# Twenty conditioning products: GpSimd scales and adds the row slices of the weights, TensorE only sums over partitions

## The reference

```python
for i in range(DEPTH):                     # DEPTH = 2
    mod_l = silu(c) @ ada_w[i] + ada_b[i]      # c: 1 x 1024, ada_w[i]: 1024 x 6144
    mod_c = silu(c_ctx) @ ada_w[i] + ada_b[i]
    sh1_l, sc1_l, gt1_l, sh2_l, sc2_l, gt2_l = split(mod_l, 6)   # and so for mod_c
    ...
```

## Time and profile before

| | us |
|---|---|
| median of 3 runs | 3075.93 |
| lowest, highest | 3074.19, 3077.70 |
| profiled execution, its span | 3075.3 |
| PE busy in it | 2984.1 |
| DVE busy | 1734.7 |
| ACT busy | 715.3 |
| GpSimd (POOL) busy | 77.7 |

### The profile page before, as it was taken

One profiled execution on the slowest core, in us unless ns is written; L12 is line 12 of the kernel. 1 busy time (PEld: TensorE's weight loads), 2 busy tenths in 40 slices (PEclk: granted clock), 3 DMA queues, 4 the chain that ended last, 5 costly groups with the idle time before them and its releaser, 6 DMA issues. The chain is left out here.

```text
span 3075.3 us, 53460 instructions
## 1 busy us (share of the span) xinstructions
PE 2984.1 (97%) x23086; PEld 2376.8 (77%) x23086; DVE 1734.7 (56%) x2567; ACT 715.3 (23%) x1371; POOL 77.7 (3%) x105
## 2 busy tenths in 40 slices
PE   8999999999999999999999999989999999999998
PEld 8988775559987998685558985655888887766897
DVE  5554456446556564464546556584333664486666
ACT  2102114222112101223322104282111012254210
POOL 1000000000001000000000000000000000001000
PEclk9999999999999999999999999999999999999999
DMA  8645403237656746313227744102222443231553
GB/s 288 223 175 184 142 30 110 97 110 234 206 183 196 260 164 216 134 60 108 99 83 234 237 141 151 55 1 83 82 82 83 150 154 113 98 122 63 165 165 110
DMA packets 279818, 429.94 MB, mean 140 GB/s; under 512 B 10072, under 2 KB 147776, under 8 KB 279584
## 3 DMA queue, kind: packets, MB, share of 16 engines
q1 hardware_dynamic: 273936, 411.52, 39.5%
q0 software_dynamic: 5024, 13.82, 1.4%
q10 hardware_dynamic: 624, 1.19, 0.1%
HBM read 425.45 MB, written 1.05 MB: 139 GB/s over the span
## 5 line engine op out<-in xcount | busy, mean ns | idle before, releaser
L460 PE MATMUL bank<-arena 64*64 64x64 f32 (+8 forms) x7292 | 740.9, 281 | 23.3 <-DVE arena L2069 4.6
L460 PE MATMUL bank<-xT,ring 128*128 128x128 f32 (+2 forms) x4512 | 725.1, 320 | 10.3 <-DVE arena L852 5.7
L460 PEld LDWEIGHTS bank<-arena 128*128 128x128 f32 (+3 forms) x7292 | 640.6, 161 | 120.1 <-issue 36.6
L460 PEld LDWEIGHTS bank<-xT,ring 128*128 128x128 f32 (+1 forms) x4512 | 657.7, 191 | 71.2 <-issue 10.5
L460 PE MATMUL bank<-ring,xT 128*128 128x512 f32 (+3 forms) x1648 | 577.2, 519 | 2.2 <-DVEq L2086 1.2
L460 PEld LDWEIGHTS bank<-ring,xT 128*128 128x128 f32 (+1 forms) x1648 | 264.0, 182 | 253.5 <-issue 237.0
L460 PE MATMUL bank<-ring,arena 128*128 128x256 f32 (+1 forms) x1584 | 436.9, 427 | 12.4 <-issue 5.3
L460 PEld LDWEIGHTS bank<-ring,arena 128*128 128x128 f32 x1584 | 298.2, 190 | 123.9 <-issue 82.0
L852 DVE TENSOR_TENSOR arena<-arena,bank 128x256 f32<-128x256 f32 (+1 forms) x198 | 92.2, 466 | 395.7 <-PE bank L460 254.7
L763 ACT COPY arena<-bank 128x256 f32<-128x256 f32 (+1 forms) x264 | 107.7, 408 | 747.2 <-PE bank L460 745.9
L812 DVE TENSOR_TENSOR arena<-ring,arena 128x1024 f32<-128x1024 f32 (+1 forms) x216 | 257.1, 1190 | 7.4
(11 more groups left out here) (421 smaller groups left out, 2186.8 us busy)
## 6 DMA issues: line engine op xcount, KB each, us to landing
ring<-in_ffn_w SPq DMA_DIRECT2D x88, 1024.0 KB, 8.0
ring<-in_w_in SPq DMA_DIRECT2D x32, 2048.0 KB, 7.7
ring<-in_ffn_w_in SPq DMA_DIRECT2D x44, 1024.0 KB, 6.5
arena<-in_ada_w SPq DMA_DIRECT2D x20, 2048.0 KB, 13.2
ring<-in_ffn_w SPq DMA_DIRECT2D x16, 2048.0 KB, 7.9
ring<-in_ffn_w_out SPq DMA_DIRECT2D x12, 2048.0 KB, 7.8
ring<-in_hgrn_w_in SPq DMA_DIRECT2D x12, 2048.0 KB, 7.9
ring<-in_ffn_w SPq DMA_DIRECT2D x8, 1536.0 KB, 6.6
```

The costliest lines, as they stand in the source:

```text
L460: return self.e.matmul(o, lhsT, rhs, start=start, stop=stop, skip_group_check=True)
```

## The change

Twenty products (still "home") get another form. For each half of the weights (four k) GpSimd multiplies the row slice k by silu(c)[k], a per-partition scalar out of `c_wide`, and adds it to a sum; the same for silu(c_ctx), if that row is needed (`ada_streams`: 14 of the 20 products need both, 6 one). PE then only sums over the partitions: 4 matmuls per row, with `pick` as weights (a column of ones among zeros, 32 columns wide). The sums lie alternately in the arena and in `xT`. The weights come in two halves, each reloaded when GpSimd has used it (`ada_half_used`); GpSimd raises `ada_summed` when a sum is complete, and waits for `ada_used` of the product two before. Marks and loads are redistributed: 3, 4, 4 and 5 products in the passes, 1, 2 and 1 in transitions; the four ring products stay in the transitions. The loads of halves follow `HOME_LOADS`: half h of a product is issued by SP h blocks after its number. GpSimd's program gets `pool_ada` in the passes; inputs of the mixer's second layer and of the embedding are issued behind the first sum of their pass. `ada_rows` has three buffers, and several semaphores are merged (`late_norms_landed`, `rows_landed`, `dve_step`).

```diff
-             "pick": (np.arange(15)[None, :] == 7) & (p >= 0),
+             "pick": (np.arange(63)[None, :] == 31) & (p >= 0),
...
-        ada_landed = sem("ada_landed")
+        ada_landed = [sem(f"ada_landed{h}") for h in range(2)]
+        ada_half_used = [sem(f"ada_half_used{h}") for h in range(2)]
+        ada_summed = sem("ada_summed")
...
+                def loaded():
+                    for h in range(2):
+                        if len(mine) - 1 - h in marks:
+                            modulation(h)
...
-                    if b in marks:
-                        modulation()
+                    loaded()
                 for half in range(2 * streams):
                     for k0 in range(0, FT, 8):
                         mine.append(blocks[0])
                         load((0, 0, k_rows(w_down, 512 * (half % 2), 512)[:, k0:min(k0 + 8, FT)]))
...
+                        loaded()
...
-            def modulation_at_home():
-                l2, c0 = next(ada)
-                if homes[0]:
-                    eng.wait_ge(ada_used, homes[0])
-                homes[0] += 1
-                eng.dma_start(f_ada[:], k_rows(a["ada_w_2"][l2], c0, 512)).then_inc(ada_landed, 16)
+                    m = next(ring_blocks)
+                    wide(a["ada_w_2"][m // 12], m % 12 * 512, 512)
+
+            def modulation_half(h):
+                m = ADA_HOME[homes[h]]
+                if homes[h]:
+                    eng.wait_ge(ada_half_used[h], homes[h])
+                homes[h] += 1
+                eng.dma_start(f_ada[:, 4 * h:4 * h + 4], k_rows(a["ada_w_2"][m // 12], m % 12 * 512, 512)[:, 4 * h:4 * h + 4]
+                              ).then_inc(ada_landed[h], 16)
...
-        ada_rows = at(arena_cols - 2 * P, 2, P)
-        ln_rows = at(arena_cols - 3 * P, P)
-        lb_rows = at(arena_cols - 3 * P, P)
-
-        IN_TRANSITION = ((2, 0, 1, 0), (2, 0, 0, 0))
-        IN_FFN = (((3, 5, 7, 8, 9), (3, 5, 7, 9)), ((3, 5, 7, 8, 9), (3, 5, 7, 8, 9)))
-        assert all(n % 2 == 0 or not m for t in IN_TRANSITION for n, m in enumerate(t))
-        assert sum(sum(n) for n in IN_TRANSITION) + sum(len(m) for n in IN_FFN for m in n) == ADA_BLOCKS
+        ada_rows = at(arena_cols - 3 * P, 3, P)
+        ln_rows = at(arena_cols - 4 * P, P)
+        lb_rows = at(arena_cols - 4 * P, P)
+
+        IN_FFN = (((5, 7, 9), (3, 5, 7, 9)), ((3, 5, 7, 9), (3, 5, 7, 9, 10)))
+        TRANSITION = ((("home", "ring", "ring"), (), ("home", "home"), ()), (("home", "ring", "ring"), (), (), ()))
+        HOME_LOADS = ((2, 4, 6, 8), (0, 2, 4, 6, 8, 10), (0, 2, 4, 6, 8), (0, 2, 4, 6, 8))
+        ADA_KINDS = [kind for l in range(DEPTH) for n in range(2)
+                     for kind in ("home",) * len(IN_FFN[l][n]) + TRANSITION[l][2 * n]]
+        ADA_HOME = [n for n, kind in enumerate(ADA_KINDS) if kind == "home"]
+        ADA_RING = [n for n, kind in enumerate(ADA_KINDS) if kind == "ring"]
+        assert len(ADA_KINDS) == ADA_BLOCKS and len(ADA_HOME) == sum(len(x) for x in HOME_LOADS)
+
+        def ada_streams(i):
+
+            n = ADA_HOME[i]
+            return (0, 1) if n // 12 == 0 or n % 12 < 4 else (0,)
+
+        def ada_sum(i, s):
+
+            if i % 2:
+                return xT[:, 4 + 2 * s:6 + 2 * s, SEQ:512]
+            return f_ada_sum[:, s].rearrange("p (a b) -> p a b", a=2)
+
+        ada_scaled = xT[:, 2:4, SEQ:512]
+
+        def pool_ada(pool, f, after_first=None):
+
+            e = pool.e
+            pool.wait_ge(x_sums, x_sums_before(f) + 1)
+            first = sum(len(x) for x in HOME_LOADS[:f])
+            for i in range(first, first + len(HOME_LOADS[f])):
+                if i >= 2:
+                    pool.wait_ge(ada_used, i - 1)
+                streams = ada_streams(i)
+                for h in range(2):
+                    pool.wait_ge(ada_landed[h], pool.due(ada_landed[h], 16))
+                    for k in range(4 * h, 4 * h + 4):
+                        w_ = f_ada[:, k].rearrange("p (a b) -> p a b", a=2)
+                        scaled = []
+                        for s in streams:
+                            last = s == streams[-1]
+                            out_ = ada_sum(i, s) if k == 0 else w_ if last else ada_scaled
+                            if last and len(streams) == 2:
+                                pool.wait_ge(pool_step, scaled[0])
+                            e.tensor_scalar(out_, w_, c_wide[:, k, s:s + 1], None, ALU.mult).then_inc(pool_step, pool.up(pool_step))
+                            scaled.append(pool.sent(pool_step))
+                        for s in streams:
+                            if k:
+                                pool.wait_ge(pool_step, scaled[s])
+                                acc = ada_sum(i, s)
+                                e.tensor_tensor(acc, acc, w_ if s == streams[-1] else ada_scaled, ALU.add
+                                                ).then_inc(pool_step, pool.up(pool_step))
+                        if k:
+                            pool.wait_ge(pool_step, pool.sent(pool_step) - len(streams) + 1)
+                    pool.wait_ge(pool_step, pool.sent(pool_step))
+                    pool.sem_inc(ada_half_used[h], pool.up(ada_half_used[h]))
+                pool.sem_inc(ada_summed, pool.up(ada_summed))
+                if i == first and after_first:
+                    after_first()
 
         def pe_ada_product(pe, home=False):
 
             if home:
-                pe.wait_ge(ada_landed, pe.due(ada_landed, 16))
-                blk = f_ada
-            else:
-                blk = pe.block()
+                pe.wait_ge(ada_summed, pe.due(ada_summed))
+                pe.wait_ge(to_act.freed, to_act.next_free())
+                bank = to_act.free_bank()
+                streams = ada_streams(pe.homes)
+                for s in streams:
+                    for j in range(4):
+                        mm = pe.mm(bank[32 * j:32 * j + 32, 0:P], pick[:, 31 - s:63 - s],
+                                   ada_sum(pe.homes, s)[:, j // 2, j % 2 * P:j % 2 * P + P], s == 0, s == streams[-1])
+                mm.then_inc(to_act.filled, 1)
...
+                pe.homes += 1
+                return
...
         def act_parameters(act):
+            act_ada_turn(act)
             act.sem_inc(ada_ready, act.up(ada_ready))
...
+            pool.wait_ge(late_norms_landed, pool.due(late_norms_landed, 48))
...
+            def mix_inputs(l):
                 if l:
                     pool.wait_ge(ln_used, pool.due(ln_used))
                 ln(l, 0)
-                pool_mix(pool, l)
+                pool_mix_rows(pool, l)
+
+            def embedding_inputs(l):
+                pool.wait_ge(ln_used, pool.due(ln_used))
+                ln(l, 2)
+                if l == DEPTH - 1:
+                    pool_second_inputs(pool)
+                pool_ple(pool, l)
+
+            for l in range(DEPTH):
+                if l == 0:
+                    mix_inputs(0)
+                pool_ada(pool, 2 * l, (lambda: mix_inputs(l)) if l else None)
+                pool_mix_lora(pool, l)
                 pool_gla(pool)
                 pool_gdn(pool)
-                for n in range(1, 4):
-                    if n > 1:
-                        pool.wait_ge(ln_used, pool.due(ln_used))
-                    ln(l, n)
-                    if n == 2:
-                        if l == DEPTH - 1:
-                            pool_second_inputs(pool)
-                        pool_ple(pool, l)
+                ln(l, 1)
+                pool_ada(pool, 2 * l + 1, lambda: embedding_inputs(l))
+                pool.wait_ge(ln_used, pool.due(ln_used))
+                ln(l, 3)
```

101 lines of the change are left out of this document (46 added, 55 removed).

## The result

The changed kernel takes 3365.9 us (median of 4 runs, 3361.4 to 3371.0) against 3075.2: a ratio of 1.094, 95% interval 1.093 to 1.096. It is slower by 291 us, and above the upper end of the predicted range (3260).

A forecast was written before the change was run, and what follows sets the result against it. PE's instruction stream, busy 97%, was taken as the bound, with PE then waiting at marks for GpSimd's sums: 3075.3 - 26.3 + 139.3 = 3188.3 us profiled, 3189 as the median of runs; range 3060 to 3260.

The forecast's parts named there:

- The scaling's price: GpSimd's scaling of 128x512 was taken at 0.65 us, so a two-row product alone at 28.8 us.
- (a): Rival: GpSimd keeps ahead, a two-row product under 26 us and not held by DVE; 3050 to 3065 us, chance 0.17.
- The port: GpSimd and DVE exclude each other at SBUF, making a two-row product 36.5 us against marks 25.9 us apart.
- the mixer's inputs: In the third pass their DMA issues and a memset behind GpSimd's first sum take 10.7 us.
- PE's gain: Shorter home products on PE save 39.5 us at marks, less 11.9 and 1.3: 26.3 us.
- the same work where PE and DVE don't wait: 0, up to 1 us: Other edits, such as late norms, wider pick, row buffers and the moved last turn, cost 0, up to 1 us.
- SP's order: Ring blocks wait in SP's queue behind unused halves; hidden in the 36.5 us while GpSimd is the bound.
- no charge: The two products in the transition after the second pass have some 93 us, need about 89, and cost nothing.
- Pass by pass: New waits of PE in the four feed-forward passes: 23.6, 44.4, 53.3 and 18 us, sum 139.3 us.
- The restart: PE may restart slowly after a long wait, but inside intervals that GpSimd sets.
- (b): Rival: GpSimd is not held by DVE but needs 28.8 us per two-row product; 3094 us, chance 0.12.
- if scalings measure 0.9 us or more, the top of the range: Sign for GpSimd's scalings: at 0.9 us or more the time would be at the range's top, 3260 us.

The follow-up runs named there:

- x5: The changed kernel with GpSimd's scalings multiplying by the constant 0.5 instead of a per-partition scalar read from SBUF: 3341.9 us, ratio 1.086.
- x13: The changed kernel with most scalings cut to 192 of their 512 columns, number and order of operations kept: 3245.4 us, ratio 1.055.
- y1: The kernel before, with four of the five products of the fourth pass summed by DVE with fused multiply-adds: 3074.75 us, ratio 0.9998.
- x1: The changed kernel with GpSimd's scalings after the first slice and all additions replaced by memsets of about equal length: 3274.6 us, ratio 1.064.
- x2: The changed kernel with GpSimd handling only the first of the eight row slices of each product: 3056.5 us, ratio 0.993.
- x4: The changed kernel with the halves of the conditioning weights loaded by GpSimd's own queue instead of SP's: 3390.4 us, ratio 1.102.
- x14: The changed kernel with the load of the second pass's last product two blocks later in SP's order: 3353.9 us, ratio 1.091.
- x8: The changed kernel with 56 idle matmuls on PE ahead of its wait for each home sum: 3452.6 us, ratio 1.123.

## Why the prediction was wrong

**The scaling's price: the step that failed.** "I take 0.65", between a memset (0.54) and the addition (1.10), as an operation that reads one tensor should lie between one that reads none and one that reads two. It takes 1.56 us alone, above the bound that the sum called its upper one, and the x5 run puts nearly all of it down to the operation itself. The addition, 1.10 in the earlier trace rows, takes 1.27 here, as the two in the earlier trace rows did (1.26, 1.27), which the sum had in hand and didn't use. One slice then takes 5.65 us (65.80 to 71.45 in the timeline) and a two-row product alone 8 x 5.65 - 2.5 (the first slice has no additions) + 0.6 (gaps) = 43.3 us for 28.8: 14.5 us more, eleven times, 160 us. All of it is the scaling's, 16 x 0.91 = 14.6: the additions are 2.4 us dearer than in the sum, and the waits of GpSimd for its own last instruction, 3.0 in the sum, are 0.6. Of the 177 us between the forecast and the result (3365.9 - 3188.9) that leaves 17. x13 shows the same from the other side: with the scaling at 0.76 us the kernel is 120 us faster. The bounds were drawn from the count of tensors read; neither row was of that operation, and the upper end should have gone beyond the nearest of them.

The Trainium skill (GPSIMD Engine Reference, "Engine selection") has GpSimd about two times slower than VectorE in two-input operations and roughly at line rate in one-input ones. The first half agrees with this case: GpSimd's addition of 128x512 takes 1.27 us where DVE's takes 0.69. The second half does not: the one-input scaling is slower than the two-input addition, and DVE does the same 128x512 scaling in 0.49 us in y1. Rival (a), beside which the prediction set that rule, would have needed 0.54.

**The port: right in kind, some 2 us too dear in size.** DVE's subtractions at 1.51 us for 1.23 and GpSimd's operations a microsecond longer behind them show that it holds both ways, which before only the earlier trace rows suggested for one. The Trainium skill (SBUF — State Buffer, "Who interferes with whom") says that a VectorE instruction with two SBUF inputs contends with a GpSimd one that reads SBUF, and calls the shared ports an exclusive lock; the single pairs in the timeline agree (81.26 to 84.82, where each operation ends 1.1 us after the one of the other engine that began before it), while in sum DVE's busy time grew by only 135 us and GpSimd's operations by some 110. The sum had 7.7 us of port per interval. The intervals, but for the one with the mixer's inputs, are 48.1 to 50.4 us, so 5 to 7 over the 43.3. In x13, where GpSimd's own time is nearer to the sum's, they are 5 to 10 over its 32.3 (37.5 to 42.0). Over the whole kernel it is some 91 us (after less x1), a third of the loss, or a dozen more as said at x1.

**PE's gain: 20.8 for 26.3.** The two-row product is 0.65 us busy and the gain in the passes 29.3 for 27.6. The miss is behind the passes, 9 us for 1.3: "the same work where PE and DVE don't wait: 0, up to 1 us" left out that PE would wait 1.5 us for ACT behind two passes and restart at the lower clock (0.50 behind the first, x2).

**SP's order: right at the marks, missed at the end of f1.** The sum gave the two transition products "some 93 us" and a need of 89, "no charge". With the true price they need 2 x 49, and while GpSimd sums the first, the loads of the second stand in SP's queue ahead of the down part's blocks, which no mark hides: the stretch is 21 us longer than that of f2 (120.5 against 99.0). x4 and x14 show the cause.

**Pass by pass.** Predicted 23.6, 44.4, 53.3 and 18 us of new waits. With 14.5 for each mark of the first three (3, 4, 4) and the 21 of f1 that is 67, 123, 111 and 18; over x2 it is 68.8, 119.0, 105.0 and 20.7. So two terms carry the miss. That the fourth pass comes out near its 18 is luck: in x13, with the scaling near the price that the sum took, it costs 3.7, so the 18 was too much for a scaling of 0.65, and at 1.56 a wait of 7.6 us at its last mark, among others, fills it. The mixer's inputs stand where the sum had them: the interval behind the first mark of f2 is 59.6 us, some 11 over its neighbours (48.5, 48.3).

**The restart** after a wait for a sum was to fall inside intervals that GpSimd sets, and x8 shows it there.

**The rivals.** (a) needed under 26 us, (b) 28.8 alone; with 43.3 neither had a chance. The line "if scalings measure 0.9 us or more, the top of the range" named the right cause, but by the sum itself the top, 3260, is a scaling of 1.05 us ((3260 - 3189) / 11 / 16 = 0.40 over 0.65), a third below what it takes.

## What to carry to other kernels

Before work goes to an idle engine, find a row of that very operation on that engine, and where there is none, let the range reach well past the price of its nearest relative. An engine that feeds another at fixed marks is judged by the time it needs for one piece against the distance of the marks, and the excess is paid at each mark, however idle that engine was before. A load held back in an in-order queue is hidden only as long as a later wait covers it: look at the stretch behind the last mark.

## What the runs showed of the hardware

- GpSimd, float32, 128 partitions: scaling by a per-partition scalar 1.56 us for 512 elements and 0.76 for 192, so some 2.5 ns an element over 0.28 (an estimate from the two); the scalar operand is 0.05 to 0.07 of it (x5). Addition of two tensors 1.27 us for 512. Memset 1.52 us for 1700 elements and 1.17 for 1280 (x1), and DVE's subtractions beside it keep their 1.23.
- DVE does the same scaling in 0.49 us and a fused multiply-add in 0.75 to 0.77 (y1).
- GpSimd and DVE with their inputs in SBUF hold each other: a GpSimd operation behind a subtraction is 1 us longer, a subtraction behind one of GpSimd's 0.8 to 0.95 (timeline of the changed kernel, 76.98 to 84.82).
- A DMA issue of a half (128 x 4 x 512) costs GpSimd 0.81 us of its own time (x4).
- After 13.4 us of idle PE the granted clock was 0.52 for the next 4 us, and 32 weight loads took 5.00 us for 3.65; with idle matmuls in the wait they took 3.65 (x8). After a wait of only 1.5 us, with one of 0.9 and one of 0.4 in the 4 us before it, it was 0.50 for 5.6 us, and 24 matmuls took 5.49 us for 2.84 (x2).
